# State-space stage in blocks of four tokens, with tables made in the first feed-forward stage

## What is computed

```python
def s5_mixer(u, lam_re, lam_im, log_dt, b_re, b_im, c_re, c_im, d_skip, w_glu, b_glu):
    lam = lax.complex(jnp.minimum(lam_re, -1e-4), lam_im)
    lam_bar = jnp.exp(lam * dt)                     # decay of one token
    b_bar = ((lam_bar - 1.0) / lam)[..., None] * lax.complex(b_re, b_im)
    ...                                             # 128 groups of 16 channels, 64 complex states each
        bu = jnp.einsum('bcgi,gpi->bcgp', u_c, b_bar)
        _, states = lax.associative_scan(combine, (a_elem, bu), axis=1)
        y = jnp.einsum('bcgp,gip->bcgi', states, c_mat).real
    ...
    z = jax.nn.gelu(y + d_skip * uf)
    out = z * jax.nn.sigmoid(z @ w_glu + b_glu)
```

## Time and profile before

| | |
|---|---|
| three runs, median (least to most) | 4101.12 us (4098.51 to 4108.22) |
| the profiled execution | 4105.02 us, span 4103.7 us |
| TensorE, matmuls | busy 3800.0 us, 93% |
| VectorE | busy 2565.8 us, 63% |
| ScalarE | busy 1822.4 us, 44% |
| GpSimd | busy 1533.1 us, 37% |

### The profile page before, as it was taken

How to read it: one execution, slowest core, us unless ns; L and a number is a source line. 1 busy time by engine, 2 the same in 40 slices (tenths; PEclk the granted TensorE clock), 3 DMA queues, 4 the chain that set the end, 5 groups by cost and what they waited for, 6 DMA issues and landing times.

```text
span 4103.7 us, 63063 instructions
## 1 busy us (share of the span) xinstructions
PE 3800.0 (93%) x26602; PEld 3228.2 (79%) x26602; DVE 2565.8 (63%) x3645; ACT 1822.4 (44%) x2919; POOL 1533.1 (37%) x725
## 2 busy tenths in 40 slices
PE   5898999999999999989999999998359989999998
PEld 3787888777877887888788888887348878888887
DVE  0435643795368897668664454688985966454457
ACT  1435443654355444545533333442654553343334
POOL 0332443143323440014344444444764434444443
PEclk8999999999999999999999999999679999999999
DMA  9653665345533451034454545453015435554543
GB/s 392 267 214 141 262 241 208 150 177 199 222 151 144 166 190 69 22 121 175 159 186 183 193 180 201 178 204 114 1 63 200 173 141 185 185 190 182 198 178 135
DMA packets 53483, 711.79 MB, mean 173 GB/s; under 512 B 5968, under 2 KB 8144, under 8 KB 10832
## 3 DMA queue, kind: packets, MB, share of 16 engines
q1 hardware_dynamic: 47664, 684.15, 44.3%
q0 software_dynamic: 3472, 21.50, 1.4%
q10 hardware_dynamic: 2064, 2.10, 0.1%
HBM read 705.63 MB, written 2.10 MB: 172 GB/s over the span
## 4 chain that ended last, share of the span: by engine, by line
PE 76%; DVE 15%; ACT 5%; DMA 2%; issue 1%; POOL 1%; SPq 0%; DVEq 0%; ACTq 0%; another core or an unknown queue 0%; POOLq 0%
PE ps L366 43%; PE ps L367 22%; DMA ring<-in_ada 2%; DVE pieces L319 2%; PE ps L2226 2%; PE ps L786 2%; ACT pieces L303 2%; DVE opa L567 1%; DVE r L1169 1%; PE ps L1896 1%; DVE scr L3426 1%; DVE scr L3422 1%; DVE scr L3428 1%; PE ps L1040 1%; PE ps L640 1%
## 5 line engine op out<-in xcount | busy, mean ns | idle before, releaser
L366 PE MATMUL ps<-opa,pieces 128*128 128x512 f32 x6192 | 2254.0, 407 | 64.4 <-DVE pieces L319 45.3
L337 POOL TENSOR_TENSOR pieces<-ring,pieces 128x1024 fp32r<-128x1024 f32 x539 | 1350.2, 2505 | 2227.5 <-ACT pieces L303 2227.4
L367 PE MATMUL ps<-opa,pieces 128*128 128x256 f32 x6192 | 1742.6, 281 | 0.0
L303 ACT ACTIVATE pieces<-ring 128x1024 fp32r<-128x1024 f32 (+1 forms) x1110 | 1098.5, 1036 | 851.5 <-PE ps L367 851.0
L366 PEld LDWEIGHTS ps<-opa,pieces 128*128 128x128 f32 x6192 | 1173.4, 189 | 358.7 <-issue 49.3
L367 PEld LDWEIGHTS ps<-opa,pieces 128*128 128x128 f32 x6192 | 1179.7, 191 | 9.0 <-issue 5.3
L366 PE MATMUL ps<-opb,pieces 128*128 128x512 f32 x2560 | 907.5, 396 | 16.5 <-DVE pieces L319 11.7
L319 DVE TENSOR_TENSOR pieces<-ring,pieces 128x1024 fp32r<-128x1024 f32 (+1 forms) x571 | 709.2, 1242 | 273.3 <-ACT pieces L303 270.9
L367 PE MATMUL ps<-opb,pieces 128*128 128x256 f32 x2560 | 725.1, 283 | 0.0
L366 PEld LDWEIGHTS ps<-opb,pieces 128*128 128x128 f32 x2560 | 482.3, 188 | 137.1 <-issue 16.2
L367 PEld LDWEIGHTS ps<-opb,pieces 128*128 128x128 f32 x2560 | 482.8, 189 | 0.1
(11 more groups left out here) (416 smaller groups left out, 3427.8 us busy)
## 6 DMA issues: line engine op xcount, KB each, us to landing
ring<-in_up SPq DMA_DIRECT2D x64, 2048.0 KB, 7.7
ring<-in_down SPq DMA_DIRECT2D x64, 2048.0 KB, 7.7
ring<-in_win SPq DMA_DIRECT2D x56, 2048.0 KB, 7.7
ring<-in_ada SPq DMA_DIRECT2D x48, 2048.0 KB, 12.0
ring<-in_wout SPq DMA_DIRECT2D x24, 2048.0 KB, 7.7
ring<-in_evin SPq DMA_DIRECT2D x18, 2048.0 KB, 7.8
ring<-in_evout SPq DMA_DIRECT2D x8, 2048.0 KB, 7.7
ring<-in_xkv SPq DMA_DIRECT2D x8, 2048.0 KB, 7.7
```

The lines of the kernel that those rows point to most:

```text
L303: a.do.activation(K.parts_of(p)[0][:, s, :], w[:, s, :], ACT.Copy).then_inc(*K.hi.up((p, h)))
L337: g.do.tensor_tensor(lo[:, s, :], w[:, s, :], hi[:, s, :].bitcast(F), ALU.subtract).then_inc(*K.lo2.up(p))
L366: pe.do.matmul(b[:, 0:512], hi[:, k, :], op[:, 512 * k:512 * k + 512], start=i == 0, stop=False)
L367: t = pe.do.matmul(b[:, 0:256], lo[:, k, :], half(op, 0, k), start=False, stop=i == kt - 1)
```

## The change

Blocks of four tokens take the place of blocks of two: 16 steps, each with four groups by 64 blocks. Each block needs tables of the output matrix times powers 0 to 3 of the decay, and of the input matrix times powers 1 to 3. These seven tables are made beside the tiles of the first feed-forward stage: constants first (`dve_s5_columns`, `act_s5_columns`, the same operations on 64 columns as before, and two products of 2048), then a table in six turns of VectorE (`dve_s5_table`), a turn being one up or down tile, then four padded pieces of it by ScalarE, two copies of 512 elements each (`act_s5_pads`), each piece stored to DRAM from GpSimd's queue (512 KB). In odin GpSimd's queue loads tables back for four direct products; SP's queue loads the rest during the state-space stage, ahead of the slabs that lend their places. The first input product runs before odin's last tile. The two differences of a step become one on VectorE; scan of step n-1 comes after the two products of step n. GpSimd makes the angles alone, in four operations. Gelu comes after all rotation tables. The functions `dve_s5_consts` in its old form, `dve_s5_lambda_c`, `act_s5_turn`, the transposes and `pool_s5_loads` are removed; reduction and parts order tokens by fours.

The diff, cut to its core (kept lines and added ones; removed lines are in the functions printed above). SP, and the feed-forward stage:

```diff
+            sp_s5_tables(K)
         if i in K.lent5:
-            sp.wait_ge(*K.prod.of(("y5", 31)))
+            sp.wait_ge(*K.prod.of(("y5", 15)))
         sp.do.dma_start(K.ring[:, i % RING, 0:n], src).then_inc(*K.landed[i % RING].up(i, 16))
...
             side = None if q + n else pe_totals(K, ("nf", l))
             pe_tile(K, p + n, K.opa, ("nf", l, "h"), (K.dve, ("usum", l, q, n)), side, 6)
+            if l == 0 and q == 0 and n in (8, 12):
+                pe_s5_rows(K, n // 4 - 2)
...
             if q:
                 a.wait_ge(*K.tile.of(K.first["down", l, q - 1] + 15))
             act_part(K, K.opb, ("ho", l, q), n, s)
+            next(tables, None)
         p = K.first["down", l, q]
+        if q == 3 and l == 0:
+            drain(tables)
+            kept_all(K, a)
         for n in range(17):
...
+            elif n < 16:
+                next(tables, None)
...
+            next(tables, None)
             dve_normed(K, p + n, h, K.rstd, ("usum", l, q, n)).then_inc(*K.dve.up())
...
         p = K.first["down", l, q]
+        if q == 3:
+            drain(tables)
...
+            elif q < 3:
+                next(tables, None)
...
+TABLES = [("c", k) for k in range(4)] + [("b", k) for k in range(1, 4)]
+TURN0 = 16
...
+def first_turn(j):
+    return TURN0 + 8 * j + 12 * (j >= 4)
...
+def act_s5_columns(K):
     a = K.a
+    dt, lr, x, th, ex, ph2, sh, d1, r, em, r2 = K.t5c
+    a.do.activation(dt, K.col("ldt"), ACT.Exp).then_inc(*K.act.up("dt"))
...
+    for _ in range(4):
+        yield
     a.wait_ge(*K.dve.of("ph"))
     a.do.activation(ex, x, ACT.Exp).then_inc(*K.act.up())
     a.do.activation(em, x, ACT.Tanh, scale=0.5).then_inc(*K.act.up())
+    a.do.activation(K.lim5, th, ACT.Sin).then_inc(*K.act.up())
     a.do.activation(sh, th, ACT.Sin, scale=0.5).then_inc(*K.act.up("sh"))
...
+    tt(fi, fi, ph2, ALU.mult, "fi")
+    yield
+    yield
+    v.wait_ge(*K.prod.of(("row5", 0, 1)))
+    tt(rows_of(K.wide5), over(lim), side, ALU.mult, ("wide5", 1))
...
+def dve_s5_table(K, j):
+    v = K.v
+    which, k = TABLES[j]
+    dst, src = table_at(K, j), table_at(K, j + 1)
...
+    if which == "c":
+        over = lambda a: a[:, :, None].broadcast_to([P, 64, 16])
+        a, b = (over(K.lre5), over(K.lim5)) if j else (over(K.fr5), over(K.fi5))
...
+    for c in range(2):
+        v.do.tensor_tensor(dst[c], src[c], a, ALU.mult).then_inc(*K.dve.up())
+        yield
+        for h in range(2):
+            s = slice(g // 2 * h, g // 2 * h + g // 2)
+            v.wait_ge(*K.dve.now())
+            v.do.tensor_tensor(T, src[1 - c][:, s], b[:, s], ALU.mult).then_inc(*K.dve.up())
+            v.wait_ge(*K.dve.now())
+            v.do.tensor_tensor(dst[c][:, s], dst[c][:, s], T, ALU.add if c else ALU.subtract).then_inc(*K.dve.up(("table", j)))
+            yield
...
+def act_s5_pads(K, j):
...
+    which, k = TABLES[j]
+    a.wait_ge(*K.dve.of(("table", j)))
...
+    for u in range(4 * j, 4 * j + 4):
+        s = u % 4
+        if u >= 2:
+            a.wait_ge(*K.kept[u % 2].of(("kept", u - 2)))
+        else:
+            a.wait_ge(*K.prod.of(("row5", 1, 1)))
+        to = K.pad5[u % 2]
+        for q in range(2):
...
+            a.do.activation(o, i, ACT.Copy, scale=K.half5[which == "b"][:, q:q + 1]).then_inc(*K.act.up(("pad", u)))
+            yield
...
+def pe_s5_rows(K, c):
...
+    pe.wait_ge(*K.dve.of(("wide5", c)))
+    pe.wait_ge(*K.dve.of("fold5"))
...
+        for m in range(8 * h, 8 * h + 8):
+            t = pe.do.matmul(b[:, 64 * (m - 8 * h):64 * (m - 8 * h) + 64], K.wide5[:, P * m:P * m + P], K.fold5, start=True, stop=True)
+        t.then_inc(*K.prod.up(("row5", c, h)))
...
+def act_s5_beside(K):
+    yield from beside(act_s5_columns(K), *(delayed(first_turn(j) + 7, act_s5_pads(K, j)) for j in range(7)))
...
+def dve_s5_beside(K):
+    yield from beside(dve_s5_columns(K), *(delayed(first_turn(j), dve_s5_table(K, j)) for j in range(7)))
...
+def pool_s5_beside(K):
+    g, p = K.g, K.first["up", 0, 0]
+    store = {first_turn(u // 4) + 7 + 2 * (u % 4) + 3: u for u in range(28)}
+    for t in range(2, 128):
+        if t in store:
+            pool_s5_store(K, store[t])
+        if t == first_turn(3) + 17:
+            g.wait_ge(*K.act.of(("pad", 15)))
+            g.do.dma_start(K.T5[0], K.D["s5bc"]).then_inc(*K.load["s5b"].up("s5b", 16))
+        pool_feed(K, p + t)
```

Odin and its queues (`load_k` loads 2 MB and 512 KB, `load_b` 512 KB and 1.5 MB, `load_c` 2 MB; `kept_all` waits for the last stores):

```diff
+def pool_odin(K):
+    g, p = K.g, K.first["odin"]
+    kept_all(K, g)
+    load_k(K, g, 2)
+    pool_feed(K, p)
+    g.wait_ge(*K.tile.of(p - 1))
+    load_k(K, g, 3)
+    pool_feed(K, p + 3)
+    g.wait_ge(*K.prod.of(("K", 2)))
+    load_k(K, g, 0)
+    pool_feed(K, p + 6)
+    g.wait_ge(*K.prod.of(("K", 3)))
+    load_k(K, g, 1)
+    pool_feed(K, p + 11)
+    g.wait_ge(*K.prod.of(("K", 1)))
+    load_b(K, g, 0)
+    pool_feed(K, p + 12)
+    pool_s5_angle(K, 0)
+    pool_feed(K, p + 14)
+    pool_s5_angle(K, 1)
+    pool_feed(K, p + 15)
...
+def sp_s5_tables(K):
+    sp = K.sp
+    kept_all(K, sp)
+    sp.wait_ge(*K.tile.of(K.first["odin"] + 15))
+    load_b(K, sp, 1)
+    load_c(K, sp, 1)
+    sp.wait_ge(*K.prod.of(("z5", 3)))
+    load_b(K, sp, 2)
+    sp.wait_ge(*K.prod.of(("y5", 3)))
+    load_c(K, sp, 2)
+    sp.wait_ge(*K.prod.of(("z5", 7)))
+    load_b(K, sp, 3)
+    sp.wait_ge(*K.prod.of(("y5", 7)))
+    load_c(K, sp, 3)
+ORDER_K = {1: 2, 4: 3, 8: 0, 10: 1}
...
+def pe_odin(K):
+    for n in range(16):
+        side = None if n else pe_totals(K, ("nm", 1))
+        pe_tile(K, K.first["odin"] + n, K.opa, ("nm", 1, "h"), (K.dve, ("us", n)), side, 6)
+        if n in ORDER_K:
+            pe_s5_direct(K, ORDER_K[n])
+        if n == 14:
+            K.pe.wait_ge(*K.act.of(("K", 1)))
+            pe_s5_in(K, 0)
...
+def pe_s5_direct(K, s):
...
+    pe.wait_ge(*K.load["kc%d" % (s % 2)].of(("kc", s)))
+    pe.wait_ge(*K.act.of(("bt", s)))
...
+    for m in range(4):
+        for c in range(2):
+            for q in range(4):
+                t = pe.do.matmul(b[32 * q:32 * q + 32, 96 * m:96 * m + 96], B[:, c, 4 * m + q, :], C[:, 0:3, 4 * m + q, c, :],
+                                 start=c == 0, stop=c == 1)
+    t.then_inc(*K.prod.up(("K", s)))
...
+def pool_s5_angle(K, m):
+    g = K.g
     if m == 0:
+        g.wait_ge(*K.prod.of(("K", 1)))
+        g.wait_ge(*K.load["io5"].of("io5"))
     else:
```

The state-space stage:

```diff
 def pe_s5(K):
+    for s in range(5):
+        if 0 < s < 4:
+            pe_s5_in(K, s)
+        if s == 1:
+            K.pe.wait_ge(*K.dve.of(("u", 15)))
+        if s:
+            pe_s5_out(K, s - 1)
+def pe_s5_in(K, s):
     pe = K.pe
+    pe.wait_ge(*K.load[LOADED_B[s]].of(("tb", s)))
+    pe.wait_ge(*K.dve.of(("u", 4 * s + 3)))
+    bs = []
+    for q in range(4):
+        if s == 1 and q == 1:
+            pe.wait_ge(*K.dve.of(("u", 15)))
+        bs.append(pe_bank(K, K.z5b, ("z5", 4 * s + q), (K.dve, ("m1", 4 * s + q))))
+    B = K.TB[s % 2].rearrange("p (k m c t) -> p k m c t", k=4, m=4, c=2)
+    for m in range(4):
+        for c in range(2):
+            for r in range(4):
+                for q in range(4):
+                    q0 = 32 * q
+                    t = pe.do.matmul(bs[q][:, 256 * c + 64 * m:256 * c + 64 * m + 64], B[q0:q0 + 32, 3 - r, m, c, :],
+                                     K.U[q0:q0 + 32, 4 * s + m, 64 * r:64 * r + 64], start=r == 0, stop=r == 3)
+    t.then_inc(*K.prod.up(("z5", 4 * s + 3)))
...
+def pe_s5_out(K, s):
...
+    pe.wait_ge(*K.act.of(("K", 1)))
+    if s:
+        pe.wait_ge(*K.load["tc%d" % (s % 2)].of(("tc", s)))
+    pe.wait_ge(*K.dve.of(("p", 4 * s + 3)))
+    pe.wait_ge(*K.gps.of(("p", 4 * s + 3)))
+    C = K.TC[s % 2].rearrange("p (k j c i) -> p k j c i", k=4, j=16, c=2)
+    direct = K.K5.rearrange("p (m k i) -> p m k i", m=16, k=3)
+    for m in range(4):
+        y = K.bank["y5", s, m // 2][:, 256 * (m % 2):256 * (m % 2) + 256]
         for z in range(4):
...
+            for q in range(4):
+                pe.do.matmul(y[32 * q:32 * q + 32, 192:256], C[:, 0, 4 * m + q, z // 2, :],
+                             K.p5[4 * s % 8 + q][:, 256 * z + 64 * m:256 * z + 64 * m + 64], start=z == 0, stop=z == 3)
+        for k in range(3):
+            for q in range(4):
+                q0 = 32 * q
+                pe.do.matmul(y[q0:q0 + 32, 64 * k:192], direct[q0:q0 + 32, 4 * s + m, k, :], K.U[q0:q0 + 32, 4 * s + m, 0:192 - 64 * k],
+                             start=k == 0, stop=False)
+        for r in range(3):
+            for z in range(4):
+                for q in range(4):
+                    t = pe.do.matmul(y[32 * q:32 * q + 32, 64 * r + 1:64 * r + 64], C[:, r + 1, 4 * m + q, z // 2, :],
+                                     K.p5[4 * s % 8 + q][:, 256 * z + 64 * m:256 * z + 64 * m + 63], start=False, stop=r == 2 and z == 3)
+        if m % 2:
+            t.then_inc(*K.prod.up(("y5", 4 * s + m)))
...
 def dve_s5(K):
...
+            v.do.tensor_tensor(M[:, 512:1024], b, c[:, 256:768], ALU.mult).then_inc(*K.dve.up(("m2", n)))
```

(30 more changed lines are left out.)

521 lines of the change are left out of this document (217 added, 304 removed).

## The result

Changed kernel: median 4120.5 us (4117.1 to 4122.5, 5 runs); the kernel before, beside it: 4101.7 (5 runs). Ratio 1.0035, 95% interval 1.002 to 1.005. I had forecast 4087. The profiled execution after has a span of 4119.2 us against 4103.7: 15.5 us more where my sum said 14.5 less, so 30 us are to be explained.

The account below looks back on a forecast made before the run. VectorE was taken to bound the state-space stage and TensorE the feed-forward tiles; +60.4 +18.3 -12.7 -80.5 = -14.5 gave 4087 us against the median 4101.1, range 4033 to 4120.

Parts of the forecast that it names:

- part 1: Feed-forward up tiles, rounds 1 and 2: table steps and ScalarE copies lengthen the chain, +60.4 us.
- part 2: Feed-forward up tiles, round 0: constants moved there from odin cost +18.3 us.
- part 3: Odin: without constants its tiles fit, direct products and first input product are added; 103.8 us, -12.7.
- part 4: State-space stage: 16 steps of 5.5 us, TensorE late in between and at the end; 119.2 for 199.7, -80.5.
- Both rivals with room in this stage: Feed-forward stage: steps fit idle time (25 instead of 78.7, 4033, chance 0.2); VectorE first at ports (63, 4071, 0.1).
- Down tiles at 0: Feed-forward down tiles: no ScalarE part hangs on VectorE there, so table steps cost 0 us.
- the 2 us for the start: Odin: an allowance of 2 us for its start, added on TensorE.
- The step that failed: State-space TensorE products: 4.5 us an input product, 13.5 an output product.
- The rival on weight loads: Input products: weight loads run in a row, 14.2 us each; odin +9.7, state-space stage +19.4; 4116, chance 0.13.
- The end of the range: Whole kernel: slowest time of the forecast range, 4120 us, set by the last rival.
- late loads: Odin: transfers issued by GpSimd come late, four products by 8 us each; 4119, chance 0.07.

Follow-up runs that it names:

- placed: late_both plus an earlier fourth scan, 37 of 42 table steps on down tiles, and constants cut into pieces; 4042.1 us (0.9842 of the kernel before).
- late_both: Changed kernel with, in up tiles, VectorE's table step moved behind its second part and ScalarE's copies before its part of the hidden tile; 4077.4 us (0.9931).
- q_outer: Changed kernel with the input product's loops swapped, row tiles outside the four of a sum; 4195.9 us (one run).
- warm: placed with unread matmuls filling TensorE's waits before the second input product and the last output product; 4043.2 us (0.9846).

## Why the prediction was wrong, point by point

All terms are differences of the two profiled executions, in us:

| term | forecast | measured |
|---|---|---|
| up rounds 1 and 2 (part 1) | +60.4 | +30.6 + 26.8 = +57.4 |
| down rounds 0, 1, 2 | 0 | +1.0 + 0.6 + 6.1 = +7.7 |
| constants in up round 0 (part 2) | +18.3 | +25.1 |
| odin (part 3) | -12.7 | -12.8 |
| state-space gap (part 4) | -80.5 | -64.2 |
| ahead of this stage / behind the gap | 0 | -3.2 / +5.4 |
| sum | -14.5 | +15.4 |

- **Part 1 was right, in mechanism and size.** A tile with step and copy takes 8.37 us (forecast 8.1), GpSimd's operation goes ahead of the table product, the step 1.8 (1.95), the copy 0.57 (0.55). Both rivals with room in this stage fall. What the argument did not ask was whether the order could be another: the same step behind the second part costs 0.66.
- **Down tiles at 0 was right for the tile and wrong for the seam.** By "seam" I mean the change from up to down tiles. After an up round that ends on steps the pieces of weights run late, and the first three down tiles of round 2 take 8.0, 7.7 and 7.3 us for 5.6, which is all of the 6.1. In placed, where up rounds 1 and 2 hold no steps and the first down tiles do, no down tile of these rounds takes more than 6.4.
- **Part 2 was a quarter too small.** Priced as the operations' own durations, 18.3 instead of 25.1. The bursts also meet GpSimd's operation: in late_both the constants of one turn show three operations of 64 columns in 2.80 us, for 0.74 in the earlier trace rows. Cutting them up gave 10 us back.
- **Part 3 was right as a sum.** The input product took 7.4 instead of 4.5, the direct products 1.53 each instead of 1.8, and the 2 us for the start did not come: errors of +2.9, -1.1 and -2.0 that cancel. The near hit of the sum is luck. The tables were in time here.
- **Part 4 failed, and decided the sign.** Its structure held: TensorE late at steps 8 and 12, the last output product bare, 6.3 us behind it. From VectorE's first step (2937.43) step 8 started at 53.0 (forecast 47.5), step 12 at 86.3 (73), and the end came at 127.9 (111.5). In these links VectorE was 7.3 better than forecast; the two input products were 12.0 worse (11.2 and 9.8 for 4.5 each) and the three output products 11.8 worse (16.8, 18.5 and 17.0 for 13.5). Of these 23.8, 14.5 are stops for "issue" inside them. Without stops the output products are 1.7 above forecast in all, and the input products take 8.1 to 8.5.
- **The step that failed** is the price of TensorE's products in part 4: "If rounds go by columns streamed: 64 x 0.058 = 3.7 ... I take 4.5" and the 13.5 of an output product, with nothing in either for stops. Rounds of the input product do not go by columns streamed: they take 112 ns at full clock and 213 at half with 32 columns as with 64, so a product takes 7.4 us at full clock. And the stops were put at nothing without a reason; they are 14.5 us on the path, the larger part of the 23.8. In the state-space stage of before, bursts of 208 records show no stop, but the row at 2826.85 of the earlier trace rows, which the prediction read for its duration, has one of 1.98 us. The rival on weight loads gave nearly the measured gap (138.6) from records one after another, which q_outer refutes for this order of the loops, so its nearness is chance.
- **The end of the range** (4120) missed the median by half a microsecond. The rival that came nearest in time, late loads (4119), did not happen in odin, which took 103.7 us. In the state-space stage TensorE did wait 7.5 us for the second input table, which SyncE asks for after odin's last tile; the forecast had no such wait. On the path it is worth little: the first output product starts 25.1 us after odin's last matmul in placed, with this wait, and in warm, where it is filled and the input product is 4.8 us shorter (26.2 in the changed kernel).

The 5.4 us behind the gap are spread over GLU, output and cross-attention projections and differ between kernels with the same code there (1,043.6 to 1,048.5 us); I leave them open.

## What to carry to other kernels

Before work is put beside a bound engine, follow the chain within one tile and choose the slot: here the same step cost 1.8 us, 0.66 or almost nothing, by its place, and the order of unchanged work took the kernel from 4120 to 4042 us. When many large matmuls are replaced by many small ones, price them by measured rounds of the same weight shape, at the clock they will run at, and by the number of instructions, not by columns. A wait for "issue" in a row of the old kernel is a price too: ask what will multiply it. Look for what produces an operand behind a wait that does not concern it, as p behind the next input product.
